# An engine's waits for itself, moved to where the next instruction depends, in the attentions, retention and memories of a four-layer transformer forward pass

## The reference

```python
def block(qi):                                  # latent attention, once per 128 queries
    s = einsum('bqhd,bkhd->bhqk', qi, k) * scale
    p = softmax(s, axis=-1)
    return einsum('bhqk,bkhe->bqhe', p, v)

# retention, each direction: scores under a decay in the distance, no softmax
scores = einsum('bnihd,bnjhd->bnhij', q, k) * decay
o = rmsnorm(o_f + o_b) ; return silu(rg) * o

# gated linear attention: the decay is a cumulated gate, per channel
A = einsum('bnihd,bnjhd->bnhij', q * exp(b - b_mid), k * exp(b_mid - b)) * mask
S = exp(b_last) * S + state_of_chunk            # carried over chunks of 64

# attention with a sink
p = exp(s - m) ; denom = exp(sink - m) + p.sum(-1) ; out = (p @ v) / denom

# mLSTM memory, each direction, then both directions are added
s   = (q @ k.T) * exp(d - m_t)                  # d: gates, causal
num = s @ v + w_inter * (q @ C) ; den = s.sum(-1) + w_inter * (q @ n)
h   = num / maximum(abs(den), exp(-m_t))
```

## Time and profile before

| | us |
|---|---|
| median of 3 runs | 2575.83 |
| lowest and highest | 2575.35, 2575.9 |
| the profiled execution | 2574.99 |
| its span in the profile | 2573.2 |

### The profile page before, as it was taken

How to read it: one execution, slowest core, us unless ns; L and a number is a source line. 1 busy time by engine, 2 the same in 40 slices (tenths; PEclk the granted TensorE clock), 3 DMA queues, 4 the chain that set the end, 5 groups by cost and what they waited for, 6 DMA issues and landing times.

```text
span 2573.2 us, 35465 instructions
## 1 busy us (share of the span) xinstructions
PE 2420.0 (94%) x13296; PEld 2001.2 (78%) x13296; DVE 1759.9 (68%) x1895; ACT 1263.5 (49%) x1465; POOL 522.4 (20%) x407
## 2 busy tenths in 40 slices
PE   7999999999999988779999979889999999999997
PEld 5658998768997855658888868577888888888886
DVE  6556874467855756468645357657888888888886
ACT  6444434544443355332222134536777777777774
POOL 1003541004522000031002520002132132232231
PEclk9999999999999998789999989888999999999998
DMA  5573553414552310025555323015989989999894
GB/s 197 198 273 140 186 181 134 164 49 147 182 202 74 112 42 1 33 88 192 194 196 197 131 69 112 18 69 226 351 336 361 347 338 361 346 341 369 334 362 175
DMA packets 71465, 503.67 MB, mean 196 GB/s; under 512 B 8192, under 2 KB 8704, under 8 KB 11264
## 3 DMA queue, kind: packets, MB, share of 16 engines
q1 hardware_dynamic: 70128, 496.75, 53.1%
q0 software_dynamic: 1168, 4.66, 0.5%
HBM read 500.33 MB, written 1.05 MB: 195 GB/s over the span
## 4 chain that ended last, share of the span: by engine, by line
PE 83%; DVE 10%; ACT 4%; issue 2%; POOL 1%; DMA 0%; DVEq 0%; ACTq 0%; SPq 0%; PEldq 0%
PE ps L424 80%; DVE ring_r L2105 1%; PE ps L464 1%; DVE h L2083 1%; POOL h_r L1353 1%; DVE h L2081 1%; DVE areaA L2075 1%; PE ps L1178 1%; DVE h L2085 1%; ACT ring_hi L1470 1%; ACT h L1548 1%; DVE areaB L2597 1%; DVE temp L2168 0%; DVE h L2682 0%; PE ps L567 0%
## 5 line engine op out<-in xcount | busy, mean ns | idle before, releaser
L1470 ACT ACTIVATE ring_hi<-ring 128x2048 fp32r<-128x2048 f32 x427 | 808.9, 1895 | 556.1 <-PE ps L424 332.3
L2854 DVE TENSOR_TENSOR ring_r<-ring,ring_hi 128x2048 fp32r<-128x2048 f32 x264 | 619.6, 2350 | 119.5 <-ACT ring_hi L1470 116.8
L424 PE MATMUL ps<-ring_hi,extra_r 128*128 128x512 f32 (+2 forms) x1808 | 610.7, 394 | 34.2 <-DVE ring_r L2105 20.4
L2105 DVE TENSOR_TENSOR ring_r<-ring,ring_hi 128x2048 fp32r<-128x2048 f32 (+3 forms) x163 | 383.1, 2350 | 192.7 <-ACT ring_hi L1470 177.8
L424 PE MATMUL ps<-extra_r,ring_hi 128*128 128x256 f32 (+1 forms) x1432 | 462.8, 323 | 22.6 <-POOL h_r L1353 21.1
L424 PE MATMUL ps<-extra_r,ring_r 128*128 128x256 f32 (+1 forms) x1432 | 458.0, 320 | 0.0
L424 PE MATMUL ps<-h_r,ring_hi 128*128 128x256 f32 (+2 forms) x1400 | 445.7, 318 | 0.0
L424 PEld LDWEIGHTS ps<-ring_hi,extra_r 128*128 128x128 f32 x1808 | 342.7, 190 | 109.4 <-DVE ring_r L2105 23.8
L424 PE MATMUL ps<-ring_r,extra_r 128*128 128x512 f32 (+2 forms) x1104 | 425.0, 385 | 0.0
L424 PEld LDWEIGHTS ps<-extra_r,ring_hi 128*128 128x128 f32 x1432 | 273.9, 191 | 46.5 <-POOL h_r L1353 24.3
L424 PEld LDWEIGHTS ps<-extra_r,ring_r 128*128 128x128 f32 x1432 | 273.9, 191 | 19.0
(11 more groups left out here) (356 smaller groups left out, 3147.9 us busy)
## 6 DMA issues: line engine op xcount, KB each, us to landing
ring<-in_experts SPq DMA_DIRECT2D x264, 1024.0 KB, 4.9
ring<-in_stream SPq DMA_DIRECT2D x202, 1024.0 KB, 4.9
ring<-in_stream SPq DMA_DIRECT2D x6, 512.0 KB, 3.6
ring<-in_stream SPq DMA_DIRECT2D x2, 576.0 KB, 3.8
res<-in_xT SPq DMA_DIRECT2D x1, 1024.0 KB, 5.8
res<-in_ctxT POOLq DMA_DIRECT2D x1, 1024.0 KB, 7.4
h<-in_consts POOLq DMA_DIRECT2D x2, 512.0 KB, 5.1
areaB<-in_cond_rows POOLq DMA_DIRECT2D x1, 1024.0 KB, 7.1
```

What stands on the lines that cost most here:

```text
L424: return pe.matmul(o, l, r, start=start, stop=stop, skip_group_check=True)
L1470: return act.activation(dst, src, ACT.Copy)
L2105: L.tell(TTN(ring_lo[:, s, 0:n], ring[:, s, 0:n], ring_hi[:, j % HIS, 0:n].bitcast(F32), ALU.subtract), "weights_lo")
L2854: TTN(ring_lo[:, s, :], ring[:, s, :], ring_hi[:, j % HIS, :].bitcast(F32), ALU.subtract).then_inc(sig("weights_lo"), 1)
```

## The change

The `Lane` gets four more ways: `go` counts the instruction on the engine's own semaphore and does not wait, `settle` waits for that count, `send` tells another engine and does not wait, `sent` waits for what was sent. `leave` releases a bank with the instruction and does not wait, `left` waits for a given bank's release. In the stages above, where the next instruction doesn't read or overwrite what the last one wrote, `step`, `tell` and `free` become `go`, `send` and `leave`. Where a named semaphore only said that a bank had been read (`att_p`, `att_pT`, `pair_p`, `pair_pT_dve`, `pair_pT_act`, `pair_oT`, `ret_sdec`, `gla_ex`, `gla_Am`, `lexp`, `ml_out`, half of `lweights`), the reader now waits for the bank's release. Two orders change besides: in `exponentials` the two exponentials out of PSUM now come before the one in SBUF, and the squares of `sum_ml` write two places in turn. The projections, the feed-forwards, the norms and the experts are as they were.

```diff
+    def go(self, ins):
+        ins.then_inc(self.order, 1)
+        self.steps += 1
+    def settle(self, but=0):
+        self.engine.wait_ge(self.order, self.steps - but)
+    def send(self, ins, name):
+        ins.then_inc(self.sig(name), 1)
+        self.told[name] = self.told.get(name, 0) + 1
...
+        def leave(ins, u):
+            ins.then_inc(bank_free[u.bank], 1)
+        def left(engine, *key):
+            u = uses[key]
+            engine.wait_ge(bank_free[u.bank], u.nth + 1)
+        def weighted(engine, l, n):
+            sq, x, d = lsteps(l)[n]
+            if d == 0:
+                engine.wait_ge(sig("lweights"), 8 * l + n // 2 + 1)
+            else:
+                left(engine, "ls", l, sq, x, len(STILES[sq]) // 2 - 1)
...
@@ PE: pv, and the memories @@
-                    pe.wait_ge(sig("pair_pT_dve"), 16 * l + 2 * j + 2)
-                    pe.wait_ge(sig("pair_pT_act"), 16 * l + 2 * j + 2)
+                    for hd in range(2):
+                        left(pe, "pair", l, "pT", 2 * j + 1, hd)
...
-                    pe.wait_ge(sig("lweights"), 16 * l + n + 1)
+                    weighted(pe, l, n)
...
@@ ScalarE: attend_pairs @@
-                        free(L, act.activation(pair_p[:, 2 * (n % 2) + hd, 0:w.keys * P], ps[:, u.bank, 0:w.keys * P],
-                                               ACT.Exp, bias=pair_neg[:, i:i + 1], scale=AD ** -0.5,
-                                               accum_out=pair_den[:, i:i + 1]), u, "pair_p")
+                        leave(act.activation(pair_p[:, 2 * (n % 2) + hd, 0:w.keys * P], ps[:, u.bank, 0:w.keys * P],
+                                             ACT.Exp, bias=pair_neg[:, i:i + 1], scale=AD ** -0.5,
+                                             accum_out=pair_den[:, i:i + 1]), u)
...
@@ ScalarE: exponentials and the squares @@
-                    L.step(act.activation(own, own, ACT.Exp, scale=-1.0))
-
                     u = uses["lm", l, n]
-                    for i in range(ns - 2):
-                        L.step(act.activation(lw[n % 2][:, i, :], ps[:, u.bank, 0:T], ACT.Exp,
-                                              bias=lc[:, STILES[sq][i], 0, d, x:x + 1], scale=-1.0))
-                    act.sem_inc(bank_free[u.bank], 1)
-                    act.sem_inc(sig("lexp"), 1)
+                    if ns > 2:
+                        for i in range(ns - 2):
+                            L.go(act.activation(lw[n % 2][:, i, :], ps[:, u.bank, 0:T], ACT.Exp,
+                                                bias=lc[:, STILES[sq][i], 0, d, x:x + 1], scale=-1.0))
+                    leave(act.activation(own, own, ACT.Exp, scale=-1.0), u)
...
-                    L.wait("ml_out", 8 * l + k + 1)
+                    left(act, "lo", l, 2 * k + 1)
+                    L.settle()
...
@@ VectorE: attend_pairs @@
-                    L.tell(STT(out=pair_neg[:, i:i + 2], in0=pair_max[:, i:i + 2], scalar=-AD ** -0.5,
+                    L.send(STT(out=pair_neg[:, i:i + 2], in0=pair_max[:, i:i + 2], scalar=-AD ** -0.5,
                                in1=rows[:, a:a + 2], op0=ALU.mult, op1=ALU.min), "pair_m")
                     if n % 2:
                         sl = slice(i - 2, i + 2)
-                        L.tell(TTN(pair_sink[:, sl].rearrange("p (t h) -> p t h", t=2),
+                        L.sent("pair_m")
+                        L.send(TTN(pair_sink[:, sl].rearrange("p (t h) -> p t h", t=2),
...
-                    free(L, copy(pair_oT[:, j % 2, :], ps[:, u.bank, 0:T]), u, "pair_oT")
+                    leave(copy(pair_oT[:, j % 2, :], ps[:, u.bank, 0:T]), u)
...
@@ VectorE: gla_qk @@
-                L.wait("gla_ex", n + 1)
+                left(dve, "gla_b", n)
-                S(TTN(y[:, 0:2, :], bc(gqk[:, x, :], 1, [P, 2, T]), e[:, 0:2, :], ALU.mult))
-                L.tell(TTN(y[:, 2, :], gqk[:, 4 + x, :], e[:, 2, :], ALU.mult), "gla_qk")
+                L.go(TTN(y[:, 0:2, :], bc(gqk[:, x, :], 1, [P, 2, T]), e[:, 0:2, :], ALU.mult))
+                L.send(TTN(y[:, 2, :], gqk[:, 4 + x, :], e[:, 2, :], ALU.mult), "gla_qk")
...
@@ VectorE: weights and heads_out of the memories @@
-                    L.wait("lexp", 16 * l + n + 1)
+                    left(dve, "lm", l, n)
...
-                        if d == 0:
-                            S(ins)
+                        if d == 1:
+                            leave(ins, u)
+                        elif i < len(STILES[sq]) // 2 - 1:
+                            L.go(ins)
                         else:
-                            free(L, ins, u)
-                    dve.sem_inc(sig("lweights"), 1)
+                            L.send(ins, "lweights")
...
                         if t == 0:
-                            S(ins)
+                            L.go(ins)
                         else:
-                            free(L, ins, us[1], "ml_out")
+                            leave(ins, us[1])
```

100 lines of the change are left out of this document (55 added, 45 removed).

## The result

The changed kernel takes 2543.95 us (median of 4 runs, 2543.66 to 2544.85) where the kernel before takes 2575.59 beside it: ratio 0.9879, 95% interval 0.9864 to 0.9895. It is 31.6 us faster. I had said 2557, 18.75 us faster, with 2547 to 2567 as the range.

What follows compares the result with a forecast made beforehand. TensorE, busy 94% of the span, was taken as the bound, so only its idle places could give. Stage terms for removed waits summed to 18.75 us, from the median 2575.83 to 2557.1, said as 2557, range 2547 to 2567.

Steps and rivals of the forecast that it cites:

- the latent attention: Latent attention stage: path mostly through waits that stay, two passes of 0.38 and 0.06 at the end, 0.8 us.
- the cut-off: All stages: waits removed between two TensorE pieces count only up to TensorE's idle time there.
- Price p: ScalarE and VectorE: a plain own wait taken away is worth 0.13 us, bounds 0.03 and 0.14.
- Price b: A bank wait with a separate count, taken away, is worth 0.25 us, bounds 0.13 and 0.27.
- Price h: Hand-over to another engine by bank release instead of a separate count: worth 0.14 us, bounds 0.06 and 0.16.
- the gated attention: Gated linear attention stage: 0.49 twice on the path to the next states, then 0.26 and 0.64; together 1.9 us.
- the retention: Retention stage: TensorE full until its tail, where a reduction, a product and a rescale lose about 0.4 us.
- the second layer's attention: Attention of layer 2: 0.35, 1.5 and 0.9 at the same prices, so 2.75 us.
- first layer's memories: Memories of layer 1: waits removed on the path of the steps, partly cut off at idle time, together 5.3 us.
- the context part: First layer's attention: VectorE would lose 1.4 us in each 5.1, but TensorE idles about 1.3, so 1.3 us.
- pair 2: Second layer's memories, second pair of steps: gain cut off at TensorE's idle time, 0.5 us.
- gain out of the clock: Rival: denser work spares half-clock stretches behind the first layer's memories, 4 us each; 2549 to 2553 us, chance 0.14.

Runs made afterwards that it cites:

- e4_waits: Changed kernel with ScalarE's and VectorE's own waits put back, hand-overs by bank release and the new exponential order kept: 2562.48 us (ratio 0.9953).
- e1_first: Kernel before with the change only in the latent attention, the retention and the gated linear attention: 2567.46 us (ratio 0.9977).
- e3_mem: Kernel before with the change only in the two layers' memories: 2559.32 us (ratio 0.9948).
- e8_warm_before: Kernel before with more warming matmuls in both layers' memories and in front of the transposes behind them: 2578.07 us (ratio 1.0014).

## Why the prediction was wrong in size

The mechanism was right: own waits and separate counts were on the path, at about the prices said. 12.9 us of the gain were not forecast, though. Of the 11.25 that the first profile shows, 3.8 are terms that I had cut off at TensorE's idle time, 5.45 are clock, for which the sum had no term, 0.9 the latent attention, and 0.56 a path that I did not see; the other terms make up the little that is left. So two steps failed: the cut-off, and a clock put at nothing in the sum. One by one:

- **Price p, right.** 0.13 us for a plain own wait: 0.12 to 0.14 in the pairs of the profile after, 0.13 in e4_waits. The rule of the Trainium skill ("VectorE: DVE Perf Modes", "The DRAIN you can't avoid"), by which a semaphore after each of eight copies costs nothing, does not carry over to these waits: 18.5 us hang on them here. The same section says that a next operation that is not held starts earlier, which I had left out; the rows agree, with starts 0.09 us ahead of the end.
- **Price b, a little low.** 0.28 between ScalarE's exponentials and 0.30 behind VectorE's copy, where I took 0.25 and had 0.27 as the upper bound. The rows with 0.23 in front of the maximum stood in the trace of before; I had priced from those with 0.15 to 0.18.
- **Price h, right only on average.** 0.19 from ScalarE to VectorE, 0.05 from VectorE to TensorE. I had read 0.06 behind one VectorE instruction and carried it over to another, whose end TensorE sees 0.15 late.
- **The terms of the gated attention (1.77), the retention (0.19) and the second layer's attention (2.71)**: within 0.25 us of 1.9, 0.4 and 2.75. For the gated attention that is partly luck: 0.5 us more came in e1_first and in the second profile, where its end does not fall at half clock. In the first layer's memories 6.1 and 5.4 came for 5.3, but only 4.5 in e3_mem.
- **The cut-off at TensorE's idle time, wrong.** This is the step that failed first. In the first layer's attention I cut the context part to 1.3 us and 4.1 came. Those 2.8 us are more than the stage's whole miss of 2.0 in the first profile; in the second it is 3.6. In the second layer's memories I cut pair 2 to 0.5 and the end to 0.45, and the waits gave 1.12 and 0.85. Two things were wrong in the context part: the idle time was 3.0 us and not 1.3, even by the gaps that the rows name (2.7), and idle time is no bound, since 1.4 us more came out of rows that count as busy. The stage's own bound from the earlier trace rows, 10.2 us of idle time for the attention, was a sum over all and never forbade 6.6.
- **The latent attention, 0.8 said and 1.68 gained.** It came as five steps of about 0.3 us, at every second unit. With ScalarE's waits back it still gains 1.18, with VectorE's 1.52, with both 0.39: here freeing either engine alone gives most of it. I had written that the path goes mostly through waits that stay, which the runs show to be too little; which instruction sets it was not settled.
- **The clock, taken as an alternative where it was an addition.** I held "gain out of the clock" against the forecast, with a chance of 0.14. It came on top: 2.15 us in the second layer's memories, 1.35 in the first FFN, 1.95 at the end. These gains are one to two us each, where that rival had 4 us from each stretch of 10. TensorE was granted half clock for about 174 us of the span before and 150 after.
- **Missed altogether:** 0.56 us in front of the gated attention's loop.

The profiled executions differ by 30.1 us and the medians by 31.6; the rest is the spread between executions. The second profile of the changed kernel gained 28.5 us. It has the 2.15 and the 1.95 again, not the 1.35, and 1.6 more in the first layer's attention. So the cut-off terms and the latent attention repeat, and of the clock's part some comes back and some moves. What remains open is which of it belongs to the change: runs with less of the change had the 1.35 and the 1.95, one of them or neither.

## What to carry over

In this kernel an own wait cost 0.13 us, and one with a separate count behind it 0.28, on the chains between ScalarE and VectorE that TensorE waits for, so take it out there wherever the next instruction does not need the result. Before cutting such a sum off at an engine's idle time, take that time from the window and not from the gaps that rows name, and compare the duration of each joined row with that of the same row where nothing holds it: busy time can shrink too. And look at the fillers: the 12 warming matmuls kept TensorE from weights that had been ready for 4.7 us before the change and for 5.0 after it, and five of them took 3.4 to 6 us less. A filler only fills if it does not need the bank whose release ends the wait.

## What the runs showed of the hardware

- Which stretches stand at half clock differs between executions of one program: of the changed kernel's two profiles one has a piece at 914.6 to 918.0 us and none in the first FFN, the other one at 233.6 to 237.1 and none in that attention. Times differ too: ten executions of e1_first span 9.5 us, while four of the changed kernel span 1.2 and four more 2.3; that the clock makes this spread was not shown. A stage whose code is unchanged differed by 2.15 us between two kernels.
- The clock does not come back at the first warming matmul: 12 of them ran at half clock (5.30 us, where 12 took 2.75 in e8_warm_before behind the memories), with 5 the step behind them still did (3.22 instead of 1.83), and with none the granted clock was 0.63 over a stretch of 98 us. Five are worth 6.4 us against none (2540.5 against 2547.0), and twelve cost 3.4 to 6 against five.
- TensorE starts 0.06 us behind the end of a VectorE product on 256 elements a partition and 0.15 us behind that of one on 512, with the same kind of signal (once in each profile of the changed kernel, twice in e4_waits). Why was not tried.
